# A two-block forward pass on one core: order of q and k in the first layer, split of the last down weights, and queues of the output

## The reference

```python
for i in range(DEPTH):                      # DEPTH = 2
    a = rms_norm(h, attn_norm[i])
    proj = a @ w_in[i]                      # q, k, v, z, xbc, dt, gq, gk, gv, gg, lr
    y_da = diff_attention(q, k, v, positions, ...)   # q, k: rms norm per head, rope, causal
    y_ssd = ssd_mixer(z, xbc, dt, ...)
    y_gla = gla_mixer(gq, gk, gv, gg, lr, ...)
    h = h + concat(y_da, y_ssd, y_gla) @ w_out[i]
    f = rms_norm(h, ffn_norm[i])
    h = h + (silu(f @ w_ffn_gate[i]) * (f @ w_ffn_up[i])) @ w_ffn_down[i]
    h = h + sigmoid(h @ ple_w_gate[i]) * (p[i] @ ple_w_proj[i])
...
h = concat(meta_tokens, x)                  # second block, 16 + 256 tokens
h = h + mixer(rmsnorm(h), w_in, ...)        # HGRN2 and RG-LRU branches
h = h + hier_moe(rmsnorm(h), ...)           # 32 experts, 2 of them per token
out = rmsnorm(h, final_g)[:, 16:]
# an expert: (silu(x @ w_gate[e]) * (x @ w_up[e])) @ w_down[e], 1024 -> 512 -> 1024
```

## Time and profile before

| | us |
|---|---|
| three runs, median (lowest to highest) | 1604.61 (1604.09 to 1605.2) |
| the profiled execution, its own time | 1602.72 |
| its span | 1600.6 |
| PE busy in it | 1570.9 (98%) |
| DVE busy | 893.3 (56%) |
| ACT busy | 194.8 (12%) |

### The profile page before, as it was taken

How to read it: one execution, slowest core, us unless ns; L and a number is a source line. 1 busy time by engine, 2 the same in 40 slices (tenths; PEclk the granted TensorE clock), 3 DMA queues, 4 the chain that set the end, 5 groups by cost and what they waited for, 6 DMA issues and landing times.

```text
span 1600.6 us, 20620 instructions
## 1 busy us (share of the span) xinstructions
PE 1570.9 (98%) x8773; PEld 1000.8 (63%) x8773; DVE 893.3 (56%) x1546; ACT 194.8 (12%) x314; POOL 36.0 (2%) x60
## 2 busy tenths in 40 slices
PE   7999999999999999999999999999999999999997
PEld 3866499984448664999744876899633333333332
DVE  3896776765558876676646676795332223121122
ACT  1321000000114110000001331410000000000001
POOL 1001000000010010000000000000000000000000
PEclk9999999999999999999999999999999999999999
DMA  6632445563525326455526333446999999999997
GB/s 199 211 112 105 164 144 180 168 195 126 207 87 182 105 106 202 128 159 177 192 105 234 133 107 132 158 165 260 378 410 427 426 425 428 426 427 425 427 422 299
DMA packets 129444, 374.68 MB, mean 234 GB/s; under 512 B 17140, under 2 KB 65592, under 8 KB 116552
## 3 DMA queue, kind: packets, MB, share of 16 engines
q1 hardware_dynamic: 118672, 370.88, 60.9%
q10 hardware_dynamic: 10680, 2.46, 0.7%
HBM read 372.28 MB, written 1.05 MB: 233 GB/s over the span
## 4 chain that ended last, share of the span: by engine, by line
PE 87%; DMA 9%; SPq 1%; DVE 1%; issue 0%; ACT 0%; POOL 0%; POOLq 0%; DVEq 0%
PE bank L858 16%; PE bank L1151 16%; PE bank L789 10%; PE bank L1588 9%; PE bank L801 6%; PE bank L1634 5%; PE bank L1404 4%; DMA weights<-in_w_down 3%; PE bank L1354 3%; DMA h<-in_w_down 3%; DMA turned_rows<-in_w_down 2%; PE bank L1276 2%; PE bank L1134 2%; PE bank L1437 2%; PE bank L1286 2%; PE bank L809 2%
## 5 line engine op out<-in xcount | busy, mean ns | idle before, releaser
L789 PE MATMUL bank<-weights,turned_rows 128*128 128x512 f32 x384 | 168.6, 596 | 1.6 <-DMA weights<-in_w_in 1.2
L3208 DVE TENSOR_TENSOR bc<-mix,bank 128x512 f32<-128x512 f32 x16 | 17.3, 1079 | 215.3 <-PE bank L1588 215.3
L858 PE MATMUL bank<-arena 128*128 128x512 f32 x296 | 133.2, 592 | 0.0
L789 PEld LDWEIGHTS bank<-weights,turned_rows 128*128 128x128 f32 x384 | 72.3, 191 | 87.8 <-issue 85.2
L1151 PE MATMUL bank<-arena 128*128 128x128 f32 x960 | 110.5, 275 | 0.0
L1151 PEld LDWEIGHTS bank<-arena 128*128 128x128 f32 x960 | 108.8, 192 | 0.0
L858 PEld LDWEIGHTS bank<-arena 128*128 128x128 f32 x296 | 56.1, 190 | 69.8 <-issue 67.8
L801 PE MATMUL bank<-turned_rows,weights 128*128 128x256 f32 x448 | 98.6, 380 | 0.0
L801 PEld LDWEIGHTS bank<-turned_rows,weights 128*128 128x128 f32 x448 | 84.7, 190 | 12.0 <-issue 0.7
L1588 PE MATMUL bank<-arena,rows_late 128*64 128x512 f32 x248 | 88.8, 596 | 0.7 <-DMA weights<-in_w_up 0.7
L1634 PE MATMUL bank<-arena,mix 128*32 128x512 f32 x480 | 80.0, 597 | 3.1 <-DMA turned_rows<-in_w_down 2.3
(11 more groups left out here) (533 smaller groups left out, 2555.3 us busy)
## 6 DMA issues: line engine op xcount, KB each, us to landing
weights<-in_w_in SPq DMA_DIRECT2D x29, 2048.0 KB, 8.0
arena<-in_w_gate SPq DMA_DIRECT2D x13, 2048.0 KB, 22.9
arena<-in_w_up SPq DMA_DIRECT2D x12, 2048.0 KB, 34.8
weights<-in_w_ffn_gate SPq DMA_DIRECT2D x22, 1024.0 KB, 5.5
weights<-in_w_ffn_up SPq DMA_DIRECT2D x22, 1024.0 KB, 8.1
weights<-in_w_ffn_down SPq DMA_DIRECT2D x10, 2048.0 KB, 7.8
arena<-in_w_down SPq DMA_DIRECT2D x10, 2048.0 KB, 30.3
weights<-in_w_up SPq DMA_DIRECT2D x9, 2048.0 KB, 20.2
```

What stands on the lines that cost most here:

```text
L789: ins = mm(b[:, :], xT[:, k, t0 + P * t:t0 + P * t + P], w[:, k, :], start=(k == 0), stop=(k == KD - 1))
L858: ins = mm(b[:, :], lhs[:, j, :], rhs[:, j, :], start=(first and j == 0), stop=(last and j == pairs - 1))
```

## The change

In layer 0, PE multiplies q0, transposes token half 1, multiplies q1, then k0 and k1, and only then transposes the two blocks of parameter rows. Layer 1 keeps its order. The last down weights come in five parts: three of two pieces, then two of one piece; the last k waits separately for each half. Of the output, SP stores the two blocks of token half 0; ACT stores token half 1 as one block of 128 x 1024, on its own queue, after DVE has scaled both halves of it.

```diff
+LAST_PARTS = ((0, 2), (2, 2), (4, 2), (6, 1), (7, 1))
...
-            in_parts(PAIRS - 1, 4, KE, lambda part, at: f"last_down{part}")
+            for e in range(2):
+                chunk_used(*LOAD_ORDER[LOAD_AT[PAIRS - 1, 4 + e] - NXS])
+            for part, (q, pieces) in enumerate(LAST_PARTS):
+                for e in range(2):
+                    at = LOAD_AT[PAIRS - 1, 4 + e] % NXS
+                    sp.dma_start(expert_slot[at][:, DE * q:DE * q + DE * pieces],
+                                 wsrc[4 + e][2 * PAIRS - 2 + e][:, DE * q:DE * q + DE * pieces]).then_inc(sem(f"last_down{part}"), 16)
...
-            for t in range(NT):
-                for half in range(2):
-                    o = 512 * half
-                    sp.wait_ge(sem(f"rows_scaled{t}"), half + 1)
-                    sp.dma_start(out[0, P * t:P * t + P, o:o + 512], xn[:, t, o:o + 512]).then_inc(sem("out_stored"), 16)
-            sp.wait_ge(sem("out_stored"), 16 * 2 * NT)
+            for half in range(2):
+                o = 512 * half
+                sp.wait_ge(sem("rows_scaled0"), half + 1)
+                sp.dma_start(out[0, 0:P, o:o + 512], xn[:, 0, o:o + 512]).then_inc(sem("out_stored"), 16)
+            sp.wait_ge(sem("out_stored"), 16 * 3)
...
-                tokens_out(T("q"), ch, [0], ahead=first_ahead if layer == 0 else lambda half: half_turned(T("n1"), 0, half))
-                tokens_out(T("k"), ch + 1, [0], ahead=lambda half: turn(T("n1"), xn, 1, "xn_ready") if half else None)
+                if layer == 0:
+                    tokens_out(T("q"), ch, [0], ahead=first_ahead)
+                    turn(T("n1"), xn, 1, "xn_ready")
+                    tokens_out(T("q"), ch, [1], ahead=lambda half: half_turned(T("n1"), 1, half))
+                    tokens_out(T("k"), ch + 1)
+                else:
+                    tokens_out(T("q"), ch, [0], ahead=lambda half: half_turned(T("n1"), 0, half))
+                    tokens_out(T("k"), ch + 1, [0], ahead=lambda half: turn(T("n1"), xn, 1, "xn_ready") if half else None)
...
-                tokens_out(T("q"), ch, [1], ahead=lambda half: half_turned(T("n1"), 1, half))
-                tokens_out(T("k"), ch + 1, [1])
+                if layer:
+                    tokens_out(T("q"), ch, [1], ahead=lambda half: half_turned(T("n1"), 1, half))
+                    tokens_out(T("k"), ch + 1, [1])
...
             for k in range(KE):
-                pe.wait_ge(sem(f"last_down{k}"), 32)
                 for half in range(2):
+                    if half == 0 or k == KE - 1:
+                        pe.wait_ge(sem(f"last_down{k + half}"), 32)
                     ins = down(PAIRS - 1, w_last, half, k, last_hidT)
...
+            act.wait_ge(sem("rows_scaled1"), 2)
+            act.dma_start(out[0, P:SEQ, :], xn[:, 1, :]).then_inc(sem("out_stored"), 16)
```

## The result

| | before | after |
|---|---|---|
| median of 6 runs each (lowest to highest), us | 1604.32 (1603.81 to 1605.2) | 1609.09 (1607.72 to 1612.31) |
| the profiled execution, its own time | 1602.72 | 1607.72 |
| its span | 1600.6 | 1605.7 |

A forecast was written before the change was run, and what follows sets the result against it. PE's own path was taken to bound the kernel, carrying early delays through to the end. +4.07 + 1.68 - 0.24 - 0.10 = +5.4 us on the 1604.61 us median gave 1610.0 us, range 1607.0 to 1611.8.

The forecast's parts named there:

- Term 1: Layer 0, first transposes of q and k: PE waits 4.8 us for VectorE, held up by late gain rows; +4.07 us.
- Term 2: After PE's stall in layer 0 the granted clock falls; +1.68 us, the loss measured at 1488 us.
- twice the measured loss: Rival: after the layer 0 stall the clock stays low twice as long; +7.1 us, 1611.7 us; chance 0.12.
- rival without loss of clock: Layer 0 stall comes but the clock does not fall; +3.7 us, 1608.3 us; chance 0.22.
- Term 3: Last down matmuls: smaller last pieces remove PE's DMA wait; -0.24 us, no more, since PE itself is next.
- Term 4: Output stores on two queues: still bound by the DMA engines, small gain from longer rows; -0.10 us.
- Only k0 is late: Rival, layer 0: late k0, not the gain rows, delays VectorE; load at 43.7, 1606.7 us; chance 0.08.
- Faster: Rival, layer 0: k-weight stall goes and VectorE is in time; -1.1 us, 1603.5 us; chance 0.06.

The follow-up runs named there:

- experiment 3: Changed kernel plus five unused matmuls on PE before the first transposes of q and k in layer 0, filling the stall; 1607.22 us, ratio 1.0022 to before.
- experiment 1: Kernel before with only the new layer 0 order of q, k and parameter rows; last weights and output as before; 1609.89 us, ratio 1.0040.
- 5: Kernel before with only the transposes of token half 1 moved into PE's wait for the k weights; 1603.24 us, ratio 0.9999.
- 6: Kernel before with only VectorE's squares of q0 and k0 moved ahead of its wait for the broadcast rows; 1603.22 us, ratio 0.9997.
- experiment 7: Kernel before with half 1's transposes in the k-weight wait and VectorE's squares ahead of the broadcast rows; 1602.75 us, ratio 0.9994.
- experiment 11: Kernel before with only the output on two queues; one execution, 1607.87 us beside 1602.98 for before.
- experiment 2: Kernel before with only the end changed: last down weights in five parts and output on two queues; 1603.48 us, ratio 0.9999.
- experiment 4: Changed kernel with the parameter-row transposes between k0 and k1 in layer 0 instead of after k1; 1607.80 us, ratio 1.0027 to before.
- 9: Kernel before with only the last down weights in five parts and a separate wait for the last half; one execution, 1604.07 us.
- 8: Kernel before with half 1's transposes in the k-weight wait, VectorE's squares earlier, and the changed end (weights, output); 1603.38 us, ratio 0.9993.
- 10: Kernel before with the changed end, but PE waits for both last weight parts before the last k; one execution, 1606.00 us.

## Why the prediction was right, step by step

**Term 1, the stall: +4.07 forecast, +3.75 measured.** Mechanism and place as put. PE restarted with q1 at 18.23 instead of 18.53, since the restart came 0.75 us after the start of VectorE's copy (17.48 to 18.23), where 0.84 had been read from another layer, and since VectorE's copy began at 17.48 instead of 17.69; so VectorE's L2395 began at 39.23 instead of 39.6. From there to PE's load it took 5.81 us against 5.76 forecast. PE's stall, 4.78, is what was said (4.8). Two readings on the way were off, without a share in the 3.75 us, which VectorE sets. The wait for the k weights was put at 1.79 us, from the first weight load alone; but two loads go out together at 18.41 and the third at 18.95, where it would have been due at 17.48 without a wait, so 1.47 us were lost. And PE's gain at the restart was 18.41 - 18.23 + 0.87 = 1.05 us, not 0.75.

**Term 2, the clock: +1.68 forecast, +1.55 measured** between the first and the second transposes (5.30 - 3.75), and 1.4 to 2.7 us by experiment 3, which alone shows the cause (1.4 by the medians against before on each chip, 2.7 against experiment 1). The mechanism was put right; the size was borrowed from the wait at 1488 us and is partly luck, as that very loss cost before next to nothing in the end. The size differs from run to run: it was 18.5 - 16.2 = 2.3 us in the profiled execution of experiment 1, so a single execution could not have settled the term. The forecast of "twice the measured loss" at 0.12 was no separate case but the upper part of this spread. The rival without loss of clock (1608.3) fell with the windows; its number would still have been inside the spread of the runs.

**Term 3, the last pieces: -0.24 forecast, -0.07 measured.** PE no longer waits for DMA in the last k: the last down takes 7.00 us where it took 1591.10 - 1583.76 = 7.34, so the wait was even worth 0.34 in that execution. But it is not in every execution: with the old four pieces the last down takes 7.11 us in experiment 1 and 7.00 in 5, 6, 7 and 11, so in four of six traces there was nothing to remove. And the pause before the sum grew from 0.05 to 0.31 us. The chain there in before, then in after:

```profile
1589.17 1.92 PE bank L1634 x16
1591.10 0.05 issue
1591.15 1.09 PE bank L1599 x3
```

```profile
1588.89 7.00 PE bank L1647 x64
1595.90 0.31 issue
1596.21 2.01 PE bank L1612 x8
```

So the term failed at "no more: PE itself is next": the wait was one of single executions, and behind it something else was next, which the trace doesn't name. In experiment 2 (0.49) the pause costs more than the wait did, and its ratio is 0.9999.

**Term 4, the output: -0.10 forecast, 0 measured.** From the start of the last scaling to the end of the span it takes 1605.7 - 1601.13 = 4.57 us, against 4.53. SP's two stores are issued from 1601.22 on and ScalarE's at 1602.05, but the DMA engines move the same bytes at the same speed, against the earlier trace rows:

```profile
1601.22 0.95 SPq L706 DMA_DIRECT2D out<-xn  x2
1602.05 0.36 ACTq L2059 DMA_DIRECT2D out<-xn  x1
```

```profile
1602.00:1604.50 2.50, 0.00 (x0) 0.00 (x0) 0.02 (x1) 0.00 (x0) 0.00 (x0) 0.50 0.99 383
```

**The sum.** 3.75 + 1.55 - 0.07 + 0.04 = +5.27, and the two executions differ by 5.0 (spans 5.1); the rest is the small net change between 63 us and the last down (5.30 to 5.13), whose cause isn't shown. That the forecast (+5.4) lies so near is partly because errors cancel: the first two terms were 0.45 us too high together and the last two 0.31 too low. That the delay is carried through, because the transfers wait for PE to free slots, held: it is 5.1 to 5.3 us at every point that I compared from 1430 us on, also where the chain goes through DMA.

**The rivals.** "Only k0 is late" fell with experiment 4, which also put a price on it: with the gain rows out of the way the load starts at 43.52 (43.7 forecast) and +0.27% stays, 1607.8 us (1606.7 forecast without a low clock, which came). "Faster" fell: VectorE would have had to be in time, and experiment 7 shows what that takes (its squares moved as well) and that it gives 0.06%, with 1 in the interval. The time that PE gained at the restart was there, 1.05 us, and of no use.

## What to carry to other kernels

Before work is moved forward on an engine, look at what the moved work was feeding: here PE pushed a small producer (two transposes of gain rows) behind 16 matmuls, and the consumer's queue, which runs in order, stood behind it. A stall on PE can cost more than its length, since the clock may fall behind it; that part varies from run to run, and here filling the stall with matmuls that nobody needs got it back. An engine that gains time at a point where two engines meet wins nothing until the other is brought forward too. And a wait of 0.3 us read from one execution may not be in the next: look at more than one trace before it is put into a sum.

## What the runs showed of the hardware

- Behind a stall of PE of 3.1 us (experiment 4) or 4.8 us the granted clock was at its lower level for about 3.4 us (after and experiment 4) to 6.9 us (experiment 1: 8 x (1 - 0.57) / 0.5), while 3 us with PE busy for only 0.75 at 1546 had left it at 1.00. It also fell where PE was busy throughout with small matmuls (128x36 to 128x128): 0.57 over 1154 to 1158 in before, 0.50 over 1156 to 1164 in experiment 11, and not in after.
- The price depends on what follows: of the 5.3 us of delay at 63 us in after, 1.55 of them the clock's, 5.1 reached the end; of the 1.7 us lost at 1488 in before, where PE next waited for DMA, at most 0.25 did.
- The pause before the last sum was 0.05 us in before and experiments 1, 3, 4, 5, 6, 9 and 11, 0.10 and 0.27 in 7 and 8, and 0.31, 0.49 and 0.93 in after and experiments 2 and 10. Experiments 3 and 4 have the changed end and no pause. In each of the five with a pause a packet of the queue of instructions moves 2.7 to 2.8 us before PE goes on; in the eight without one it is 2.9 to 4.9 us, so PE never went on sooner than 2.7 us behind it. The changed kernel has it at 1593.4 to 1593.6 (queue, packets, MB, share of 16 engines):

```profile
q8 instruction: 1, 0.02, 31.7%
```

A fetch of instructions that comes late would fit both, the pause and its coming and going between kernels whose end is the same. There is one trace of each kernel, so whether it comes with the edit or with the execution isn't known. This is a correlation, and the cause stays open.
